# Two layers' gate rows and rotary half-swap moved from constant-matrix products to DMA

## The chip, the cores and the metric

The kernel runs on one NeuronCore of a Trainium2 chip, as one program. The metric is the device time of one execution in microseconds; lower is better. All arithmetic is in 32-bit floats. The engines named here are TensorE (matrix products), VectorE, ScalarE, SyncE (which issues the weight loads) and the DMA engines.

## The reference

The model has a first block (a Hyena mixer and a gated linear scan side by side, then a mixture of 64 experts) and a second block of two hybrid layers on 256 tokens of width 1024. A hybrid layer projects its normalized input to 21 parts, runs five branches of width 512 on them, gates and merges the branches, projects again and adds the result to its input. Two of the branches are touched here.

The mLSTM branch has 4 heads of width 128. Per head and token it has a row of gate values, from a running sum `bcum` of the log of the forget gate and a running maximum:

```
bcum = cumsum(log_sigmoid(f));  m_t = bcum + cummax(i - bcum)       (chunk by chunk in the reference)
log_d[t, s] = bcum[t] - bcum[s] + i[s] - m_t[t]
sc[t, s] = (q[t] . k[s]) * d**-0.5 * exp(log_d[t, s])   for s <= t
h[t] = sum_s sc[t, s] v[s] / max(|sum_s sc[t, s]|, exp(-m_t[t]))
```

The term `bcum[t] - m_t[t]` depends on the query's token alone, and so does `exp(-m_t[t])`. The kernel holds scores with keys on the partitions and queries along the free dimension, so both of these rows have to be present on all 128 partitions.

The retention branch turns its queries and keys by a rotary embedding before it forms scores with a fixed decay:

```
rotary(t):  t1, t2 = t[..., :64], t[..., 64:]
            concat(t1 * cos - t2 * sin,  t1 * sin + t2 * cos)
```

In the kernel the 128 places of a head are the partitions, so the rotation needs each half of the partitions to see the values of the other half.

## The kernel before

Activations lie with the feature on the partitions and the 256 tokens along the free dimension. A projection to 128 columns is a strip: 8 products of 128x128 weights with 128x256 activations into one bank of PSUM (line 518). Values (`ml_v`, `rt_v` and others) are projected with tokens on the partitions instead, 128x512 at a time (line 531). A unit is 4 strips of weights, 2 MB, and SyncE loads it into one of three slots as soon as the unit three places earlier has been used (line 485).

Strips are numbered as jobs. Jobs take PSUM banks 0 and 1 in turn, and a strip starts only when the one two places before it has been taken out of its bank (`evacuated(pe, j - 2)`). For `ml_o`, `rt_q`, `rt_k`, `rt_v` and `gm_u` ScalarE takes it out (function `take`, line 774, and line 878). For `ml_z`, `rt_z` and `gm_z` ScalarE computes an exponential (`exp_neg`, line 780), and VectorE's function `gate` (lines 956 to 962) adds one, takes the reciprocal and multiplies; its last operation frees the bank.

The order of work on each engine is written out by hand in one function for each engine (`layers_pe`, `layers_act`, `layers_dve`), with semaphores between them. Both layers run the same code. Around the change TensorE's order in a layer is:

- `ml_v` 0, the input and forget gates (line 645), `ml_v` 1, the strips `ml_o` 0 to 3, a turn of the gate values into columns (line 651), then the strip `ml_z` 0.
- The front of head 0, then `ml_z` 1, 2 and 3. A front (`ml_front`) is a product of the 4 gate rows with the constant `sel` (4x128, a row of ones for one head), which puts that head's two rows on all partitions of a PSUM bank (line 666), and a pair of causal products of keys and queries into the next bank (lines 563 and 564).
- A loop over the heads: front of the next head, strip `rt_q`, sums over values and over ones (lines 568 and 569), strip `rt_k`.
- `rt_v` 0, the head norm's sums (line 687), `rt_v` 1.
- Four products with the constant `rot`, 128x128, with entries -1 and 1, on two heads of `rt_q` or `rt_k` each (line 699). They give the swapped and signed halves in four PSUM banks.
- The strips `gm_u` 0 and 1, then, when VectorE's rotation has finished, the first retention front (`rt_front`, again lines 563 and 564), `gm_u` 2 and 3, and a loop over the heads like the one above.
- The merge of the five branches: 80 gate and branch products in pairs (lines 731 and 737), and the output projection (line 752).

VectorE computes the gate rows (lines 1096 to 1105) while TensorE is in `ml_v` 1 and `ml_o`. Between the gates of `ml_z` 0 and `ml_z` 1 it forms the weights of head 0 (lines 1116 and 1117 read the broadcast row from PSUM, ScalarE takes the exponential at line 886, line 1119 multiplies by the scores). In the loop it forms the next head's weights and then the current head's quotient (lines 1130 to 1133), where the broadcast `exp` row comes from a copy that ScalarE makes of it (`ml_exm`, line 889). The scaling by the head norm follows (lines 1137, 1138), and then the rotation: four times a product with the sine into a buffer `rt_t`, a product with the cosine in place and a sum (lines 1147 to 1149). The sine and cosine (`rope`) are computed once in the first block, from the positions and the constant `inv_freq`.

All constants of this kind lie in one block `const` of 1121.5 KB, loaded at the start (line 1275), behind the input and ahead of the first weights.

Of the kernel before, what the change touches and what calls it, by code (L numbers as in the profile page):

```python
# [7 lines left out]
F32 = mybir.dt.float32  # L8
I32 = mybir.dt.int32
ALU = mybir.AluOpType  # L10
# [86 lines left out]
def shape_constants():  # L97
# [7 lines left out]
    rot = np.zeros((P, P))  # L105
    rot[np.arange(64) + 64, np.arange(64)] = -1
    rot[np.arange(64), np.arange(64) + 64] = 1
    c.add("rot", rot)
# [7 lines left out]
    c.add("inv_freq", np.concatenate([inv, inv])[:, None])  # L116
    sel = np.zeros((4, 4, P))
    sel[np.arange(4), np.arange(4)] = 1
    c.add("sel", sel.reshape(4, -1))
# [151 lines left out]
def build_program(nc, d, spot):  # L271

    with ExitStack() as ctx:
# [112 lines left out]
        rt_q, rt_k, rt_v = ly.take(4, SEQ), ly.take(4, SEQ), ly.take(2, HALF)  # L386
        ly.at = kept_at + 2 * KD * SEQ
# [44 lines left out]
        ml_w, ml_exm = lw.take(2, 3 * P), lw.take(2, SEQ)  # L432
# [3 lines left out]
        ml_sum = lw.take(2, 4)  # L436
        assert lw.at <= (RING - RING2) * WSLOT
        lw = Layout(spare, r_three)
        rt_t = lw.take(2, 2 * SEQ)
# [57 lines left out]
        def layers_pe(pe):  # L497
            for plan in plans:
# [156 lines left out]
                w("mg_e", 1, 1)  # L655
# [101 lines left out]
        def layers_act(act):  # L757
# [3 lines left out]
            for plan in plans:  # L761
# [117 lines left out]
                w("mg_r", 2, 2)  # L879
# [1389 lines left out]
```

## Time and profile before

| | |
|---|---|
| median of 3 runs | 2385.25 us (2384.37 to 2386.61) |
| profiled execution | 2390.79 us |
| its span, first to last instruction | 2389.0 us |
| TensorE products busy | 2026.9 us, 85% |
| TensorE weight loads busy | 1365.8 us, 57% |
| VectorE busy | 891.4 us, 37% |
| ScalarE busy | 282.4 us, 12% |
| data moved | 592.23 MB, mean 248 GB/s |
| mean granted TensorE clock | 0.935 of full speed |

The span is that of the profiled execution, which is a single one and is 5.5 us above the median of the timed runs. Its time is 1.8 us more than its span. The first block up to the experts takes the first slices, the expert stage lies between some 300 and 1262 us, and the two hybrid layers follow to the end. In the trace a 32-bit product appears as two records, so 8 products of a kind are counted as 16. The records of products overlap by the length of the pipeline; the time that a piece of work takes on TensorE is read from the difference of two start times.

### The profile page before, as it was taken

What the parts mean: (1) busy time and instruction counts of PE and PEld (TensorE: products, weight loads), DVE (VectorE), ACT (ScalarE), POOL (GpSimd) and SP (SyncE); (2) the same over time, 40 slices, a digit from 0 to 9 for tenths busy, and PEclk for the clock granted to TensorE, in tenths of its full rate; (3) what the DMA queues carried; (4) which work ended last, traced back from release to release, by engine and by line L of the source; (5) the groups of instructions that cost most, each with busy time, mean ns of one, the idle gap of its engine ahead of it and who ended that gap; (6) DMA issues with size and microseconds to landing.
All of it is one profiled execution on the core that took longest, in us unless ns stands there. A gap on an engine that the chain in (4) does not pass through costs nothing. (4 is left out here: it accounts for less than half of the span.)

```text
span 2389.0 us, 24442 instructions
## 1 busy us (share of the span) xinstructions
PE 2026.9 (85%) x10208; PEld 1365.8 (57%) x10208; DVE 891.4 (37%) x1479; ACT 282.4 (12%) x632; POOL 0.2 (0%) x4
## 2 busy tenths in 40 slices
PE   7999976767766666666668999999999999999998
PEld 5576752323322222222225877788885877788887
DVE  5446431111111111111113454465543244466553
ACT  1102210000000000000002221110002222111001
POOL 0000000000000000000000000000000000000000
PEclk9999988898988878888888999999999999999999
DMA  6122189999999999999994332334444233234442
GB/s 232 71 92 73 76 357 427 429 427 428 428 427 429 429 426 429 429 428 430 428 429 194 129 119 106 132 133 158 140 178 161 106 141 141 106 115 157 141 151 88
DMA packets 45194, 592.23 MB, mean 248 GB/s; under 512 B 5463, under 2 KB 6904, under 8 KB 7800
## 3 DMA queue, kind: packets, MB, share of 16 engines
q1 hardware_dynamic: 43672, 585.34, 60.9%
q10 hardware_dynamic: 1440, 5.70, 0.7%
q8 instruction: 63, 1.03, 0.2%
q14 instruction: 19, 0.16, 0.0%
HBM read 589.98 MB, written 1.05 MB: 247 GB/s over the span
## 5 line engine op out<-in xcount | busy, mean ns | idle before, releaser
L518 PE MATMUL ps<-arena,ring 128*128 128x256 f32 x1856 | 413.8, 378 | 0.1
L518 PEld LDWEIGHTS ps<-arena,ring 128*128 128x128 f32 x1856 | 345.7, 189 | 50.6 <-issue 2.9
L1591 PE MATMUL ps<-ring,arena 128*32 128x512 f32 x2048 | 250.8, 635 | 91.4 <-DMA ring<-in_w_experts 72.0
L731 PE MATMUL ps<-arena,ring 128*128 128x256 f32 x1280 | 289.2, 378 | 0.0
L1618 PE MATMUL ps<-ring,arena 128*32 128x512 f32 x1024 | 175.2, 818 | 118.1 <-DMA ring<-in_w_experts 113.4
L731 PEld LDWEIGHTS ps<-arena,ring 128*128 128x128 f32 x1280 | 241.5, 189 | 35.6 <-issue 1.0
L1591 PEld LDWEIGHTS ps<-ring,arena 128*32 128x32 f32 x2048 | 63.3, 113 | 260.2 <-issue 140.3
L1618 PEld LDWEIGHTS ps<-ring,arena 128*32 128x32 f32 x1024 | 33.2, 130 | 242.6 <-DMA ring<-in_w_experts 162.8
L737 PE MATMUL ps<-arena,ring 128*128 128x256 f32 x640 | 151.8, 379 | 0.3
L1578 PE MATMUL ps<-arena 128*128 128x128 f32 x512 | 90.6, 359 | 67.2 <-DVE arena L2124 67.2
L1176 DVE RECIPROCAL arena<-arena 128x256 f32<-128x256 f32 x80 | 140.3, 1753 | 2.8
L2139 DVE COPY arena<-ps 128x512 f32<-128x512 f32 x32 | 20.6, 686 | 306.7 <-PE ps L1618 306.7
L1338 PE MATMUL ps<-arena,ring 128*128 128x272 f32 x512 | 126.4, 404 | 6.6 <-DVE arena L1826 4.0
L737 PEld LDWEIGHTS ps<-arena,ring 128*128 128x128 f32 x640 | 121.0, 189 | 18.4 <-issue 1.0
L1578 PEld LDWEIGHTS ps<-arena 128*128 128x128 f32 x512 | 87.6, 271 | 73.4 <-DVE arena L2124 73.4
L1338 PEld LDWEIGHTS ps<-arena,ring 128*128 128x128 f32 x512 | 98.8, 195 | 33.1 <-DVE arena L1826 4.5
L1175 DVE TENSOR_SCALAR arena<-arena 128x256 f32<-128x256 f32 x80 | 23.6, 295 | 176.0 <-ACT arena L929 176.0
L1623 PE MATMUL ps<-arena 128*128 128x256 f32 x256 | 68.4, 426 | 22.5 <-DVE arena L2139 22.5
L1623 PEld LDWEIGHTS ps<-arena 128*128 128x128 f32 x256 | 53.5, 215 | 52.6 <-DVE arena L2139 44.2
L929 ACT ACTIVATE arena<-ps 128x256 f32<-128x256 f32 x80 | 30.8, 385 | 380.1 <-PE ps L731 374.4
L959 DVE RECIPROCAL arena<-arena 128x256 f32<-128x256 f32 x40 | 70.1, 1753 | 1.4
L531 PE MATMUL ps<-ring,arena 128*128 128x512 f32 x160 | 70.3, 593 | 0.0
(385 smaller groups left out, 1739.6 us busy)
## 6 DMA issues: line engine op xcount, KB each, us to landing
ring<-in_w_experts SPq DMA_DIRECT2D x192, 2048.0 KB, 25.5
ring<-in_w_layers SPq DMA_DIRECT2D x42, 2048.0 KB, 7.8
ring<-in_w_layers SPq DMA_DIRECT2D x40, 1536.0 KB, 6.5
ring<-in_w_first SPq DMA_DIRECT2D x10, 2048.0 KB, 8.3
arena<-in_w_mem SPq DMA_DIRECT2D x2, 2048.0 KB, 11.1
arena<-in_mem ACTq DMA_DIRECT2D x2, 1024.0 KB, 6.9
arena<-in_fourier SPq DMA_DIRECT2D x1, 1544.0 KB, 20.8
arena<-in_gm_rows ACTq DMA_DIRECT2D x2, 768.0 KB, 4.6
```

Source lines behind the costliest of these rows:

```text
L518: last = pe.matmul(ps[:, j % 2, 0:SEQ], t[:, s, k, :], lhs[:, k, :], start=(k == 0), stop=(k == KD - 1))
L531: last = pe.matmul(ps[:, bank_of(name, j), :], lhs[:, k, m * P:(m + 1) * P], t[:, :, k, :], start=(k == 0), stop=(k == KD - 1))
L731: last = pe.matmul(ps[:, j % 2, 0:SEQ], t[:, k, :], an[:, k, :], start=(k == 0), stop=(k == KD - 1))
L737: last = pe.matmul(ps[:, (j + 1) % 2, 0:SEQ], t[:, KD + k, :], y_all[:, n, k, :], start=(k == 0), stop=(k == 3))
L929: act.activation(esig[:, p % 2, :], ps[:, j % 2, 0:SEQ], ACT.Exp, scale=-1.0).then_inc(sem(f"job_out{j % 2}"), 1)
L959: link(dve.reciprocal(e, e))
L1176: link(dve.reciprocal(e, e))
L1338: last = pe.matmul(out, w[:, k, :], a[:, k, :], start=(k == 0), stop=(k == KD - 1))
L1578: last = pe.matmul(ps[:, 4 + k // 4, (k % 4) * P:(k % 4 + 1) * P], xn[:, tt, k * P:(k + 1) * P], onehot[:, tt, :], start=(tt == 0), stop=( ...
L1591: last = pe.matmul(ps[CAP * e:CAP * (e + 1), v // 4, :], xg[:, (v % 4) * 2 + k, CAP * e:CAP * (e + 1)], w[:, k, e, :], start=(v % 4 == 0 a ...
L1618: last = pe.matmul(ps[CAP * e:CAP * (e + 1), 2 + half, :], mid_t[:, v - 8, CAP * e:CAP * (e + 1)], w[:, e, half * 512:(half + 1) * 512], s ...
L1623: last = pe.matmul(ps[:, 4 + k // 2, (k % 2) * SEQ:(k % 2 + 1) * SEQ], y_slot[:, k * P:(k + 1) * P], back, start=True, stop=True)
```

## The change

The constants `rot` and `sel` go, with the products that use them (lines 666 and 699) and ScalarE's copy `ml_exm`.

In their place ScalarE sends, behind the evacuation of `ml_o` 0, the 4 x 512 gate rows to a buffer in DRAM, and behind that of `ml_o` 2 it waits for this transfer and issues a second one, which reads the 2048 values back on every one of the 128 partitions (`ml_all`, 1 MB). VectorE reads the rows from `ml_all` for the weights and for the quotient. TensorE's first front moves from ahead of `ml_z` 1 to behind it, and VectorE's and ScalarE's work for head 0 moves by one gate in the same way.

For the rotation ScalarE issues, once the last `rt_k` is out of its bank, two transfers from SBUF to SBUF of 512 KB each: partitions 64 to 127 of `rt_q` and `rt_k` to partitions 0 to 63 of `rt_turned`, and the other way round. VectorE's rotation works on `rt_turned`; the sign is now in `inv_freq`, whose first half is negative. TensorE waits for the rotation one strip later, behind `gm_u` 2. All new transfers are on ScalarE's queue.

```diff
-    c.add("rot", rot)
-    c.add("inv_freq", np.concatenate([inv, inv])[:, None])
-    c.add("sel", sel.reshape(4, -1))
+    c.add("inv_freq", np.concatenate([-inv, inv])[:, None])
...
+        rt_qk = arena[:, kept_at:kept_at + 8 * SEQ]
...
+        ml_all = lw.take(4, 2 * SEQ)
+        rt_turned = lw.take(8, SEQ)
+        ml_rows_out = nc.dram_tensor("ml_rows_out", (LAYERS, 4, 2 * SEQ), F32, kind="Internal").ap()
...
                 def ml_front(hd):
-                    at = 2 + 4 * (hd % 2)
-                    sel = C("sel", 4).rearrange("p (h m) -> p h m", h=4)[:, hd, :]
                     if hd >= 2:
-                        w("ml_dx", 2 * NH, 2 * hd - 2)
-                        w("ml_exm", NH, hd - 1)
                         w("ml_s", NH, hd - 1)
-                    pe.matmul(ps[:, at, :], sel, ml_rows[0:4, :], start=True, stop=True)
-                    causal_pair(ps[:, at + 1, :], lambda kt: ml_k[:, hd, kt * P:(kt + 1) * P], ml_q[:, hd, :]).then_inc(sem("mb_ps"), 1)
+                    causal_pair(ps[:, 3 + 4 * (hd % 2), :], lambda kt: ml_k[:, hd, kt * P:(kt + 1) * P], ml_q[:, hd, :]).then_inc(sem("mb_ps"), 1)
+                strip("ml_z", 1)
                 ml_front(0)
-                strip("ml_z", 1)
                 strip("ml_z", 2)
...
-                unit_evacuated(pe, plan, "rt_q")
-                unit_evacuated(pe, plan, "rt_k")
                 w("ml_h", NH, NH)
-                for i, src in enumerate((rt_q, rt_q, rt_k, rt_k)):
-                    pe.matmul(ps[:, 2 + i, :], C("rot"), xr(src[:, 2 * (i % 2):2 * (i % 2) + 2, :]), start=True, stop=True).then_inc(sem("rr_ps"), 1)
...
                 strip("gm_u", 1)
+                strip("gm_u", 2)
                 w("rt_rot", 4, 4)
                 rt_front(0)
-                strip("gm_u", 2)
...
                     act.activation(ml_o[:, i, :], ps[:, j % 2, 0:SEQ], ACT.Exp, scale=-1.0).then_inc(sem(f"job_out{j % 2}"), 1)
-                w("mg_r", 2, 2)
-                act.activation(ml_rows[0:4, SEQ:2 * SEQ], ml_rows[0:4, SEQ:2 * SEQ], ACT.Exp).then_inc(sem("mg_e"), 1)
+                    if i == 2:
+                        w("ml_rows_out", 16, 16)
+                        act.dma_start(xr(ml_all), ml_rows_out[l].rearrange("a b -> (a b)").partition_broadcast(P)).then_inc(sem("in_ml_all"), 16)
+                    if i == 0:
+                        w("mg_r", 2, 2)
+                        act.activation(ml_rows[0:4, SEQ:2 * SEQ], ml_rows[0:4, SEQ:2 * SEQ], ACT.Exp).then_inc(sem("mg_e"), 1)
+                        w("mg_e", 1, 1)
+                        act.dma_start(ml_rows_out[l], ml_rows[0:4, :]).then_inc(sem("ml_rows_out"), 16)
...
-                    if hd >= 2:
-                        w("ml_h", NH, hd - 1)
-                    act.copy(ml_exm[:, hd % 2, :], ps[:, 2 + 4 * (hd % 2), SEQ:2 * SEQ]).then_inc(sem("ml_exm"), 1)
                 exp_neg("ml_z", 0)
+                exp_neg("ml_z", 1)
                 ml_decays(0)
-                for i in range(1, 4):
+                for i in range(2, 4):
                     exp_neg("ml_z", i)
...
+                unit_evacuated(act, plan, "rt_q")
+                unit_evacuated(act, plan, "rt_k")
+                for half in range(2):
+                    act.dma_start(xr(rt_turned)[64 * half:64 * half + 64, :], rt_qk[64 - 64 * half:128 - 64 * half, :]).then_inc(sem("in_turned"), 16)
                 take("rt_v", 0, rt_v[:, 0, :])
...
-                    dve.scalar_tensor_tensor(x[:, 0:SEQ], ps[:, at, 0:SEQ], ml_col[:, hd:hd + 1], LC("causal_neg"), ALU.add, ALU.add).then_inc(sem("ml_dx"), 1)
+                    dve.scalar_tensor_tensor(x[:, 0:SEQ], ml_all[:, hd, 0:SEQ], ml_col[:, hd:hd + 1], LC("causal_neg"), ALU.add, ALU.add).then_inc(sem("ml_dx"), 1)
...
                 gate("ml_z", 0, y_all[:, 1])
+                gate("ml_z", 1, y_all[:, 1])
+                w("in_ml_all", 16, 16)
                 ml_weights(0)
...
-                    link(dve.scalar_tensor_tensor(r, den, -1.0, ml_exm[:, hd % 2, :], ALU.mult, ALU.max))
+                    link(dve.scalar_tensor_tensor(r, den, -1.0, ml_all[:, hd, SEQ:2 * SEQ], ALU.mult, ALU.max))
...
-                for i, src in enumerate((rt_q, rt_q, rt_k, rt_k)):
-                    s = src[:, 2 * (i % 2):2 * (i % 2) + 2, :]
-                    w("rr_ps", 4, i + 1)
-                    t = rt_t[:, i % 2, :].rearrange("p (h t) -> p h t", h=2)
-                    tick(dve.tensor_tensor(t, ps[:, 2 + i, :].rearrange("p (h t) -> p h t", h=2), rope[:, 0:1, :].to_broadcast([P, 2, SEQ]), ALU.mult))
+                w("in_turned", 32, 32)
+                for i in range(4):
+                    t, qk = (v.rearrange("p (h t) -> p h t", t=SEQ)[:, 2 * i:2 * i + 2, :] for v in (xr(rt_turned), rt_qk))
+                    tick(dve.tensor_tensor(t, t, rope[:, 0:1, :].to_broadcast([P, 2, SEQ]), ALU.mult))
```

## Rows read from the trace of the kernel before

**Rows 1.** The page, part 2: what the DMA engines moved in each fortieth of the span.
```profile
GB/s 232 71 92 73 76 357 427 429 427 428 428 427 429 429 426 429 429 428 430 428 429 194 129 119 106 132 133 158 140 178 161 106 141 141 106 115 157 141 151 88
```

**Rows 2.** Windows: length, busy us (instructions) by engine, TensorE's clock, DMA share, GB/s.
```profile
core 0: us, PE busy (x) PEld busy (x) DVE busy (x) ACT busy (x) POOL busy (x), PEclk, DMA share, GB/s
1450.00:1512.00 62.00, 61.94 (x270) 47.73 (x269) 28.68 (x44) 9.64 (x27) 0.00 (x0) 1.00 0.35 129
1600.00:1800.00 200.00, 200.00 (x928) 174.94 (x927) 101.25 (x140) 16.72 (x45) 0.00 (x0) 1.00 0.46 158
1995.00:2140.00 145.00, 144.94 (x617) 110.84 (x615) 72.27 (x108) 28.91 (x58) 0.00 (x0) 1.00 0.29 105
```

**Rows 3.** Timeline of TensorE, mLSTM part of layer 0: start, us, line, operands, count.
```profile
1450.90 3.72 PE L518 MATMUL ps<-arena,ring 128*128 128x256 f32 x16
...
1456.36 10.85 PE L518 MATMUL ps<-arena,ring 128*128 128x256 f32 x48
1467.14 1.12 PE L666 MATMUL ps<-ring,arena 4*128 4x512 f32 x2
...
1468.95 3.62 PE L518 MATMUL ps<-arena,ring 128*128 128x256 f32 x16
...
1483.83 3.62 PE L518 MATMUL ps<-arena,ring 128*128 128x256 f32 x16
1487.38 1.12 PE L666 MATMUL ps<-ring,arena 4*128 4x512 f32 x2
```

**Rows 4.** Timeline of TensorE, from the last `rt_k` on, layer 0.
```profile
1505.62 7.03 PE L531 MATMUL ps<-ring,arena 128*128 128x512 f32 x16
...
1521.07 3.60 PE L699 MATMUL ps<-arena 128*128 128x512 f32 x8
1524.51 7.07 PE L518 MATMUL ps<-arena,ring 128*128 128x256 f32 x32
1531.42 0.59 PE L563 MATMUL ps<-arena 128*128 128x256 f32 x2
...
1532.07 7.07 PE L518 MATMUL ps<-arena,ring 128*128 128x256 f32 x32
```

**Rows 5.** Timeline of VectorE in the same stretches of layer 0.
```profile
1438.04 0.40 DVE L1105 SCALAR_TENSOR_TENSOR ring<-ring 4x256 f32<-4x256 f32 x1
...
1458.09 0.47 DVE L1116 SCALAR_TENSOR_TENSOR ring<-ps,ring,arena 128x256 f32<-128x256 f32 x1
...
1459.41 0.55 DVE L1119 TENSOR_TENSOR ring<-ring,ps 128x384 f32<-128x384 f32 x1 [0.59 <-ACT ring L886]
1460.43 0.30 DVE L956 TENSOR_SCALAR arena<-arena 128x256 f32<-128x256 f32 x1 [0.47 <-ACT arena L780]
...
1463.01 0.42 DVE L962 TENSOR_TENSOR arena<-ps,arena 128x256 f32<-128x256 f32 x1
...
1517.97 1.23 DVE L1138 TENSOR_TENSOR arena<-arena 128x1024 f32<-128x1024 f32 x1
1522.13 0.69 DVE L1147 TENSOR_TENSOR ring<-ps,arena 128x512 f32<-128x512 f32 x1 [2.93 <-PE ps L699]
...
1529.61 0.69 DVE L1149 TENSOR_TENSOR arena<-arena,ring 128x512 f32<-128x512 f32 x1
```

**Rows 6.** Timeline of ScalarE: evacuations of `ml_o` 0 and of `rt_k` 3.
```profile
1440.11 0.38 ACT L878 ACTIVATE ring<-ps 128x256 f32<-128x256 f32 x1 [2.87 <-PE ps L518]
...
1505.82 0.37 ACT L774 COPY arena<-ps 128x256 f32<-128x256 f32 x1 [4.39 <-PE ps L518]
```

**Rows 7.** DMA issues: queue, count, KB each, median us from issue to landing.
```profile
arena<-in_mem ACTq DMA_DIRECT2D x2, 1024.0 KB, 6.9
...
out<-arena SPq DMA_DIRECT2D x4, 256.0 KB, 2.2
```

**Rows 8.** The start: load of the constants, ScalarE's squares, and TensorE's first wait.
```profile
arena<-in_const SPq DMA_DIRECT2D x1, 1121.5 KB, 8.0
...
5.83 2.02 ACT L256 ACTIVATE arena<-arena 128x2176 f32<-128x2176 f32 x1 [3.81 <-DMA arena<-in_h]
...
PE ps L261 <- DMA arena<-in_const: 9.4, 1, 9.4
```

More of the change, by code:

```diff
@@ L104, in shape_constants @@
     c.add("notbefore", i[:, None] >= i[None, :])
-    rot = np.zeros((P, P))
-    rot[np.arange(64) + 64, np.arange(64)] = -1
-    rot[np.arange(64), np.arange(64) + 64] = 1
-    c.add("rot", rot)
     c.add("keymask", np.concatenate([i[:, None] < np.arange(SEQ)[None, :], i[:, None] < i[None, :]], axis=1))
@@ L115, in shape_constants @@
     inv = (np.float32(10000.0) ** (-(np.arange(half, dtype=np.float32) / np.float32(half)))).astype(np.float32)
-    c.add("inv_freq", np.concatenate([inv, inv])[:, None])
-    sel = np.zeros((4, 4, P))
-    sel[np.arange(4), np.arange(4)] = 1
-    c.add("sel", sel.reshape(4, -1))
+    c.add("inv_freq", np.concatenate([-inv, inv])[:, None])
     c.add("run", np.broadcast_to((np.arange(T) % CHH != 0)[None], (P, T)))
@@ L431, in build_program @@
         ml_rows = lw.take(2 * SEQ)
-        ml_w, ml_exm = lw.take(2, 3 * P), lw.take(2, SEQ)
+        ml_w = lw.take(2, 3 * P)
         ml_den = lw.take(2, SEQ)
@@ L436, in build_program @@
         ml_sum = lw.take(2, 4)
+        ml_all = lw.take(4, 2 * SEQ)
+        rt_turned = lw.take(8, SEQ)
+        ml_rows_out = nc.dram_tensor("ml_rows_out", (LAYERS, 4, 2 * SEQ), F32, kind="Internal").ap()
         assert lw.at <= (RING - RING2) * WSLOT
         lw = Layout(spare, r_three)
-        rt_t = lw.take(2, 2 * SEQ)
         rt_w = lw.take(2, 3 * P)
@@ L1110, in ml_weights @@
                 def ml_weights(hd):
-                    at, x = 2 + 4 * (hd % 2), ml_w[:, hd % 2, :]
-                    w("mb_ps", NH, hd + 1)
+                    at, x = 3 + 4 * (hd % 2), ml_w[:, hd % 2, :]
                     if hd >= 2:
                         w("mo_ps", NH, hd - 1)
-                    dve.scalar_tensor_tensor(x[:, 0:SEQ], ps[:, at, 0:SEQ], ml_col[:, hd:hd + 1], LC("causal_neg"), ALU.add, ALU.add).then_inc(sem("ml_dx"), 1)
-                    dve.scalar_tensor_tensor(x[:, SEQ:3 * P], ps[:, at, P:SEQ], ml_col[:, 4 + hd:5 + hd], LC("causal_neg")[:, 0:P], ALU.add, ALU.add).then_inc(sem("ml_dx"), 1)
+                    dve.scalar_tensor_tensor(x[:, 0:SEQ], ml_all[:, hd, 0:SEQ], ml_col[:, hd:hd + 1], LC("causal_neg"), ALU.add, ALU.add).then_inc(sem("ml_dx"), 1)
+                    dve.scalar_tensor_tensor(x[:, SEQ:3 * P], ml_all[:, hd, P:SEQ], ml_col[:, 4 + hd:5 + hd], LC("causal_neg")[:, 0:P], ALU.add, ALU.add).then_inc(sem("ml_dx"), 1)
                     w("ml_de", NH, hd + 1)
-                    dve.tensor_tensor(x, x, ps[:, at + 1, 0:3 * P], ALU.mult).then_inc(sem("ml_s"), 1)
+                    w("mb_ps", NH, hd + 1)
+                    dve.tensor_tensor(x, x, ps[:, at, 0:3 * P], ALU.mult).then_inc(sem("ml_s"), 1)
                 gate("ml_z", 0, y_all[:, 1])
+                gate("ml_z", 1, y_all[:, 1])
+                w("in_ml_all", 16, 16)
                 ml_weights(0)
-                for i in range(1, 4):
+                for i in range(2, 4):
                     gate("ml_z", i, y_all[:, 1])
@@ L1141, in layers_dve @@
                 head_scale(ml_q, "mlh", y_all[:, 1], "ml_y")
-                for i, src in enumerate((rt_q, rt_q, rt_k, rt_k)):
-                    s = src[:, 2 * (i % 2):2 * (i % 2) + 2, :]
-                    w("rr_ps", 4, i + 1)
-                    t = rt_t[:, i % 2, :].rearrange("p (h t) -> p h t", h=2)
-                    tick(dve.tensor_tensor(t, ps[:, 2 + i, :].rearrange("p (h t) -> p h t", h=2), rope[:, 0:1, :].to_broadcast([P, 2, SEQ]), ALU.mult))
-                    link(dve.tensor_tensor(s, s, rope[:, 1:2, :].to_broadcast([P, 2, SEQ]), ALU.mult))
-                    dve.tensor_tensor(s, s, t, ALU.add).then_inc(sem("rt_rot"), 1)
+                w("in_turned", 32, 32)
+                for i in range(4):
+                    t, qk = (v.rearrange("p (h t) -> p h t", t=SEQ)[:, 2 * i:2 * i + 2, :] for v in (xr(rt_turned), rt_qk))
+                    tick(dve.tensor_tensor(t, t, rope[:, 0:1, :].to_broadcast([P, 2, SEQ]), ALU.mult))
+                    link(dve.tensor_tensor(qk, qk, rope[:, 1:2, :].to_broadcast([P, 2, SEQ]), ALU.mult))
+                    dve.tensor_tensor(qk, qk, t, ALU.add).then_inc(sem("rt_rot"), 1)
                     w("rt_rot", 4, i + 1)
```

2 lines of the change are left out of this document (removed).

## The prediction

> **What bounds the kernel now.** I read the page's slices first: the DMA rate stands at 427 to 430 GB/s from the sixth to the twenty-first slice, the expert stage, and at a third of that and less behind it [rows 1]. So the experts are bound by loads, and what follows is not. Then the windows of the two hybrid layers. The reader is to see there that TensorE is busy 61.94 of 62 us in the stretch with the mLSTM, all of 200 us in the merge that follows, and 144.94 of 145 us in the same stretch of layer 1, always at a granted clock of 1.00 (2.4 GHz), while VectorE, ScalarE and the DMA engines are far from full [rows 2]. So in the layers TensorE alone sets the end, and what it no longer has to do comes off the time, one for one, unless a new wait takes its place. Third, the timeline of TensorE over the instructions that the diff takes out, because there the price of each is a difference of two start times. Last, VectorE and ScalarE beside them, to see how late a transfer may land.
>
> **Units of the sum.** A plain strip is 3.455 us (two of them lie between 1524.51 and 1531.42) [rows 4]. The front of a retention head, a pair of causal products and nothing else, takes 1532.07 - 1531.42 = 0.65 us [rows 4].
>
> **The row broadcast leaves TensorE.** Now a front of an mLSTM head takes 1468.95 - 1467.14 = 1.81 us, the `sel` product with it [rows 3]. Without the product it is a retention front: 0.65 us. The strip ahead of a `sel` product is also longer, 1487.38 - 1483.83 = 3.55 against 3.455, 0.10 us [rows 3]. One `sel` product thus costs 1.26 us, and there are 4 in each layer, 8 in all. For heads 2 and 3, in the middle of the loop, I take all of it: 2.52 us a layer.
> Around heads 0 and 1 the gates of `ml_z` interfere. From the start of `ml_z` 0 to that of `rt_q` 0 it is 1468.95 - 1450.90 = 18.05 us [rows 3]. In it the three strips from 1456.36 to 1467.14 take 10.78 where 3 x 3.455 + 0.10 = 10.47 is due: 0.31 us of waiting. The place is `ml_z` 3, which needs the bank of `ml_z` 1, and that gate ends at 1463.01 + 0.42 = 1463.43 [rows 5]. In the new order: `ml_z` 0 with its present start-up 3.55, `ml_z` 1 3.455, front 0 0.65, strips 2 and 3 6.91, front 1 0.65: 15.2 us, so `rt_q` 0 could start at 1466.1. Its wait is for the gate of `ml_z` 2. Gate 1 now starts behind a strip that ends 1457.9, plus 0.3 and ScalarE's 0.4: 1458.6, and lasts 3.0 (1460.43 to 1463.43): 1461.6. The weights of head 0 are behind it, 1458.09 to about 1459.96, 1.9 us with ScalarE's exponential in their middle [rows 5]: 1463.5. Gate 2 then takes 3.0: 1466.5, and with the handshake `rt_q` 0 starts about 1466.6. That is 0.6 us of waiting in place of 0.31. The stretch falls from 18.05 to 15.8 us: 2.2 us. The unknown here is the order of ScalarE's work: below, no wait (0.6 more a layer); above, the exponential of gate 2 behind that of the weights, another 0.5.
>
> **The rotation leaves TensorE.** The four `rot` products lie from 1521.07 to 1524.51, 3.44 us, back to back [rows 4]. They go whole: TensorE has no wait in front of them.
>
> **Is the broadcast there in time?** ScalarE sends the rows after the evacuation of `ml_o` 0 at 1440.11 + 0.38 [rows 6]; with the exponential (0.4) and the issue (0.5) that is 1441.4. VectorE's part must be ready by then; its last operation on the rows ends at 1438.04 + 0.40 [rows 5], so this wait costs nothing. A store of 256 KB lands 2.2 us after issue [rows 7]; this one has 8 KB and is taken at the same 2.2: 1443.6. ScalarE asks for it two strips after 1440.11, at 1447.4: 3.8 us of room. Behind that wait stand the evacuation of `ml_o` 3 and then `ml_col`; TensorE would feel them only at `ml_z` 1. The broadcast of 1 MB is issued at 1447.4 and read by VectorE at 1461.6: 14.2 us. The same size on the same queue landed in 6.9 us as the median of two [rows 7]; taken: 7. The nearest worse case is that the 2 MB unit issued at 1450.4 goes wholly before it: 2.1 MB at 427 GB/s, 4.9 us [rows 1], so 12 us. Both ends cost nothing. If it did come later, VectorE's queue holds gate 2, for which TensorE already waits, so every microsecond beyond 14.2 is lost at once.
>
> **Are the turned parts there in time?** Let E be the end of `rt_k` 3, now 1505.62 [rows 4]. ScalarE copies it 0.2 us later for 0.37 [rows 6], then issues two transfers of 512 KB: E + 1.5. VectorE is at that time waiting for the norm of the mLSTM; the scaling ends at 1517.97 + 1.23 = 1519.20, E + 13.6 [rows 5]. The rotation takes 1529.61 + 0.69 - 1522.13 = 8.2 us [rows 5], nearly the same with an operand in SBUF (0.68 against 0.69 in the rows). TensorE reaches the first retention front at E + 15.45 (to 1521.07) + 3 strips = E + 25.8. So landing by E + 17.5 costs nothing, 16 us after issue. Expected: the loads for the slots of `rt_q` and `rt_k` are issued at about E - 4.8 and E, 4.2 MB together; at 427 GB/s they and the 1 MB take 12.3 us from about E - 2.8: E + 9.5 at the latest for a fair share, and E + 3.7 + 5 = E + 8.7 if alone. Then the rotation runs from E + 13.6 to E + 21.8, 4 us ahead of TensorE (now 1530.30 against 1531.42: 1.1 us). Bounds of the added wait: 0 at this rate, and no upper end from any row, since no copy from SBUF to SBUF is in the trace; the nearest is the slowest rival below.
> The transfers of rows 7 touch all 128 partitions, and no row shows one between halves. The Trainium skill says in "SBUF — State Buffer", section "Door 1: The DMA port swizzle", that a range of 64 partitions reaches only half the ports, measured there at 196 GB/s, and that two transfers to opposite halves serialize. By that, an estimate: 1.05 MB in 5.4 us instead of 2.5, landing up to 3 us later, about E + 12.5, still before VectorE is free. By the rule the sum is the same; what it takes is a part of the room.
> The weight loads that share with these transfers have a slot free more than ten microseconds before use, so a delay of 2.5 to 5 us does not reach TensorE.
>
> **The smaller constant block.** 128 + 512 columns leave `const`: 320 of 1121.5 KB. TensorE's first product waits for it until 9.4 us [rows 8]. At 427 GB/s that is 0.77 us; the bounds are 0 (if what is queued beside it fills the gap) and 1.5 (ScalarE's squares, ready at 5.83 + 2.02 = 7.85, bound next [rows 8]). Taken: 0.8. Everything behind in the first block hangs on that chain and moves with it.
>
> **Other edits.** ScalarE loses 8 short copies; four DMA issues of 0.5 us fall into gaps of 3 us: nothing. The sign in `inv_freq` is data.
>
> **Sum.** A layer: 2.2 + 2.52 + 3.44 = 8.2 us; two layers 16.4; start 0.8: 17.2 us. The profiled execution took 2390.79 (span 2389.0 and 1.8 around it), so 2373.6 for it. It lies 5.5 above the median of the runs, 2385.25; from that the forecast is 2368.0 us, 0.7% faster.
>
> **Rivals.**
> (1) VectorE's gate chain becomes the bound in the mLSTM part. For it: TensorE already waits 0.31 us there and each gate holds VectorE 3.0 of a strip's 3.455. Then the 4 fronts of each layer turn into waits, and only rotation and start are left, 6.9 + 0.8: 2377.5. Against it: in the loop over heads VectorE has one quotient and one set of weights, about 5 us, in what will be 8.9 us.
> (2) The broadcast is late, 3 us beyond its 14.2 (two trips through DRAM and a unit load beside it): 6 us back, 2374. Against: 1 MB never needed that long in the layers.
> (3) Slower than before: the exchange between halves of SBUF is not spread over the 16 DMA engines. Its price is in the stretch before the first retention front. On one engine, 427/16 = 26.7 GB/s, 1.05 MB takes 39.3 + 2.2 = 41.5 us, 25.3 beyond the 16.2 of room; twice: 50.6 lost, 2418.6. It decides from 24.4 us after issue on, where the 8.2 gained in a layer are gone. For it: no row shows such a copy. Against: rows of 8 KB on 64 partitions look like every other transfer, and all of those share the engines.
> (4) It does not do what it says: the waits take just what the products cost, for instance a landing near 24 us. About 2385. Nothing speaks for this exact size.
>
> **How the numbers follow.** Forecast 0.79, with a range of its own of 2365 to 2371; rival 1 0.07; rival 2 0.06; rival 3 0.04; rival 4 0.04. About 0.2%, 5 us, is what a measurement here can tell from no change. Faster: 0.79 + 0.07 + 0.06 = 0.92, of which I move 0.01 to slower for what isn't listed: 0.91; same 0.04; slower 0.05. The range goes down to 2363.5 (no wait at `rt_q` 0, 1.2; 0.6 more at the start; the rest is the spread of the runs, 2.2) and up to 2377.5, which takes rivals 1 and 2 in.
>
> **What would show it.** In the profile after: no products of 4 x 512 and no rotation products; fronts of 0.65 us; a gap of about 0.6 us ahead of `rt_q` 0; `rt_v` 1 followed at once by `gm_u`; the broadcast landing in 5 to 9 us and the two exchange transfers in 5 to 11; VectorE's rotation beginning right behind the scaling, not behind a DMA; the first product at 8.6 us. Wrong would be TensorE idle ahead of the first retention front, or VectorE's first weights released by a DMA.

## The result, and the profile after

The changed kernel takes 2367.32 us (median of 4 runs, 2366.11 to 2370.99), the kernel before 2385.56 in the same session. The ratio is 0.9925, with a 95% interval from 0.9914 to 0.9937: 18 us, or 0.75%, faster. The forecast was 2368.0, and 17.2 us. Two later sessions gave 2371.08 against 2386.65 (0.9934, 0.9917 to 0.9951) and 2369.59 against 2387.43 (0.9929, 0.9915 to 0.9943), so the gain is 16 to 18 us.

The profiled execution took 2367.8 us, with a span of 2366.0. In its timeline TensorE has lost the products of 4x512 and of the rotation. The mLSTM part of layer 0 answers to [rows 3]:

```profile
1442.62 7.17 PE L514 MATMUL ps<-arena,ring 128*128 128x256 f32 x32
1449.63 0.59 PE L559 MATMUL ps<-arena 128*128 128x256 f32 x2
...
1457.19 0.59 PE L559 MATMUL ps<-arena 128*128 128x256 f32 x2
1457.62 0.38 PE L560 MATMUL ps<-arena 128*128 128x128 f32 x2
1458.11 3.69 PE L514 MATMUL ps<-arena,ring 128*128 128x256 f32 x16
...
1492.36 7.03 PE L527 MATMUL ps<-ring,arena 128*128 128x512 f32 x16
...
1500.94 7.03 PE L527 MATMUL ps<-ring,arena 128*128 128x512 f32 x16
1507.81 10.52 PE L514 MATMUL ps<-arena,ring 128*128 128x256 f32 x48
1518.17 0.59 PE L559 MATMUL ps<-arena 128*128 128x256 f32 x2
1518.82 3.62 PE L514 MATMUL ps<-arena,ring 128*128 128x256 f32 x16
```

From `ml_z` 0 to `rt_q` 0 it is now 1458.11 - 1442.62 = 15.49 us, where it was 18.05. A front of 0.65 from 1457.19 ends at 1457.84, so TensorE waits 0.27 us for the gate of `ml_z` 2. The loop over the heads lasts 1492.36 - 1458.11 = 34.25 us, where it was 36.67 (1505.62 - 1468.95 in [rows 4] and [rows 3]). `gm_u` follows `rt_v` 1 at once. In layer 1 one thing is different: a gap of 1.81 us ahead of the first retention front, in TensorE's timeline:

```profile
2068.18 10.52 PE L514 MATMUL ps<-arena,ring 128*128 128x256 f32 x48
2080.51 0.70 PE L559 MATMUL ps<-arena 128*128 128x256 f32 x2 [1.81 <-DVE arena L1143]
```

VectorE's timeline shows why, layer 0 first and then layer 1. The rotation no longer begins behind the scaling (line 1133) but behind a DMA:

```profile
1504.71 1.23 DVE L1133 TENSOR_TENSOR arena<-arena 128x1024 f32<-128x1024 f32 x1
1509.40 0.69 DVE L1141 TENSOR_TENSOR ring<-ring,arena 128x512 f32<-128x512 f32 x1 [3.47 <-DMA ring<-arena]
...
1516.90 0.69 DVE L1143 TENSOR_TENSOR arena<-arena,ring 128x512 f32<-128x512 f32 x1
...
2065.07 1.23 DVE L1133 TENSOR_TENSOR arena<-arena 128x1024 f32<-128x1024 f32 x1
2072.26 0.69 DVE L1141 TENSOR_TENSOR ring<-ring,arena 128x512 f32<-128x512 f32 x1 [5.96 <-DMA ring<-arena]
```

In layer 0 the rotation ends at 1517.59, 0.6 us ahead of TensorE; in layer 1 it is late. Both rows with DMA in them are what the prediction didn't expect, and TensorE's gap in layer 1 is its own sign of being wrong. The issues and landings of the new transfers (issue row, then its time to landing in layer 0 and in layer 1; then the page's medians for the broadcast and the constants) are:

```profile
L900 ACTq DMA_DIRECT2D ring<-arena x2: 537/574/611, 1493.0 to 1493.6; - x2
DMA to landing us min/median/max: 12.7/14.2/15.8
...
L900 ACTq DMA_DIRECT2D ring<-arena x2: 484/549/614, 2053.4 to 2053.9; - x2
DMA to landing us min/median/max: 12.2/15.3/18.3
...
ring<-ml_rows_out ACTq DMA_DIRECT2D x2, 1024.0 KB, 4.8
...
arena<-in_const SPq DMA_DIRECT2D x1, 801.5 KB, 6.8
```

The broadcast landed 4.8 us after an issue at 1438.7, and VectorE used it at 1453.2. The exchange took 12 to 18 us, and the 2 MB load that SyncE issued 0.5 us ahead of it landed after 16.5 us in layer 0, where the load at the same place took 9.5 before; nothing waited for it. At the start TensorE's first wait ended at 8.12, not 9.37.

### Where the time between the two traces lies

The spans differ by 23.0 us, more than the timed medians, so I set stretches of both side by side. The layers are cut at the first product of the gate projection of each layer, which is the same instruction in every kernel, and at the first product of layer 1.

| stretch, us | before | after | after, 2nd trace | after, 3rd trace |
|---|---|---|---|---|
| start to the gate projection of layer 0 | 1425.91 | 1417.63 | 1422.35 | 1424.81 |
| from there to layer 1 | 387.37 | 378.95 | 378.95 | 378.95 |
| layer 1 to its gate projection | 181.34 | 181.41 | 181.58 | 181.58 |
| from there to the last product | 383.97 | 377.62 | 377.66 | 375.55 |

The two stretches that the change touches are 8.42 and 6.35 us shorter. In the third trace the exchange landed in 15.1 us in both layers, TensorE had no wait in layer 1, and its stretch is 8.42 shorter too. What lies ahead of them spreads by 7 us among executions of one kernel. A part of this is TensorE's granted clock in the first block, in windows of 12 us around the same group of products (columns as in [rows 2]), before, after, and after in its second trace:

```profile
250.00:262.00 12.00, 9.36 (x40) 7.50 (x39) 3.79 (x11) 5.08 (x12) 0.00 (x0) 0.72 0.00 0
```
```profile
246.00:258.00 12.00, 9.36 (x60) 8.07 (x59) 6.51 (x15) 5.87 (x14) 0.00 (x0) 1.00 0.00 1
```
```profile
250.00:262.00 12.00, 9.36 (x42) 7.54 (x41) 3.95 (x11) 4.93 (x12) 0.00 (x0) 0.72 0.00 0
```

The same kernel stands at 1.00 once and at 0.72 once, so the 3 us that this gives are no effect of the change. The place is behind a gap of 2.64 us, which all fourteen traces of this case have: the 16 products behind it take 3.8 us in four of them, 5.2 to 5.5 in three and 6.8 in seven, whatever the kernel.

### The profile page after: what moved, and what is told of

Read it like the earlier page. It is cut to its first block and busy times, and to the rows that moved or that the text cites. A ratio compares the mean times of both kernels' runs of the same rounds, so it can differ in the third digit from the quotient of the medians.

```text
span 2366.0 us, 24364 instructions
## 1 busy us (share of the span) xinstructions
PE 2004.5 (85%) x10176; PEld 1359.0 (57%) x10176; DVE 891.0 (38%) x1479; ACT 279.7 (12%) x624; POOL 0.2 (0%) x4
## 5 line engine op out<-in xcount | busy, mean ns | idle before, releaser
L723 PEld LDWEIGHTS ps<-arena,ring 128*128 128x128 f32 x640 | 121.0, 189 | 18.4 <-issue 1.0
L1617 PE MATMUL ps<-arena 128*128 128x256 f32 x256 | 69.1, 429 | 22.5 <-DVE arena L2133 22.5
L2130 DVE TENSOR_TENSOR arena<-arena,ps 128x512 f32<-128x512 f32 x16 | 11.0, 689 | 159.0 <-PE ps L1585 159.0
## 6 DMA issues: line engine op xcount, KB each, us to landing
arena<-in_w_mem SPq DMA_DIRECT2D x2, 2048.0 KB, 11.2
```

Of the source, the lines that this page charges most:

```text
L723: last = pe.matmul(ps[:, (j + 1) % 2, 0:SEQ], t[:, KD + k, :], y_all[:, n, k, :], start=(k == 0), stop=(k == 3))
L1617: last = pe.matmul(ps[:, 4 + k // 2, (k % 2) * SEQ:(k % 2 + 1) * SEQ], y_slot[:, k * P:(k + 1) * P], back, start=True, stop=True)
```

## The experiments

Theory A was that the gain is what TensorE no longer does, less the idle time that the late exchange gives back. Theory B put a part of it down to the clock ahead of the layers. For the landing of the exchange there were three theories: S, it shares the DMA engines with the unit loads; H, a transfer on 64 partitions is slow by itself; E, it runs on few engines. Where a single execution of a kernel is given, there is no interval.

### The change again, its two parts alone, and the constants

The first is the changed kernel itself.

> The changed kernel as it is, on the chip of the next three. Theory A: the gain is TensorE's products taken off, 8.4 us in each layer by the two traces, less TensorE's idle time ahead of the first retention front (0 in layer 0, 1.9 us in layer 1), plus 1.3 to 2 us at the start; so 18 us below the kernel before, 2367 us, and a trace that shows this idle time in layer 1 again, with the exchange landing 12 to 18 us after issue. Rival B: part of the 18 us is the granted clock in stages that the change does not touch (5 us of the 23 us between the two traces); then this time lies at 2370 to 2372 us, and the idle time may be gone.

Gate rows by DMA alone:

```diff
 # from the changed kernel
...
+    c.add("rot", rot)
-    c.add("inv_freq", np.concatenate([-inv, inv])[:, None])
+    c.add("inv_freq", np.concatenate([inv, inv])[:, None])
...
+                for i, src in enumerate((rt_q, rt_q, rt_k, rt_k)):
+                    pe.matmul(ps[:, 2 + i, :], C("rot"), ...)
...
-                    act.dma_start(xr(rt_turned)[...], rt_qk[...])
...
```

VectorE's rotation reads the products from PSUM again, and TensorE's wait for it stands behind `gm_u` 1 again.

> The gate rows by DMA, the rotation by products as before (its constant and its sign back). Theory A: the stretch from ml_z 0 to rt_q 0 falls from 18.05 to 15.5 us, the loop over the heads from 36.67 to 34.25, both layers: 10.0 us; the constants shrink by 256 KB: 1 us; the time is 11 us below the kernel before, 2374.5 us. Rival B: the wait for the gate of ml_z 2 takes most of it: 8 us or less. With no exchange in flight TensorE has no idle time ahead of the first retention front beyond that of before.

Exchange by DMA alone:

```diff
 # from the kernel before
...
-                    pe.matmul(ps[:, 2 + i, :], C("rot"), ...)
...
+                for half in range(2):
+                    act.dma_start(xr(rt_turned)[...], rt_qk[...])
...
```

The sign in `inv_freq`, VectorE's rotation and the later wait of TensorE go with it; `sel` and its products stay.

> The exchange by DMA, the gate rows by the constant product as before. Theory A: 3.44 us less on TensorE in each layer, less 0 to 1.9 us of idle time where the exchange lands too late, plus 0.2 us for 64 KB of constants: 5 to 7 us below before, 2378.5 to 2380.5 us; with rows_only it adds up to the whole change within 1.5 us. Rival B: the two edits help each other, because the broadcast delays weight loads which then meet the exchange: then the exchange lands clearly sooner here, under 9 us after issue, and no idle time is left.

The constants at their old size:

```diff
+    c.add("unused", np.zeros((P, 5 * P)))
```

> The changed kernel with 640 unused columns in the constant block, so that it has its old 1121.5 KB. Theory A: TensorE's first product waits until 9.3 us instead of 8.1, and all behind it moves: 1.3 us slower than the changed kernel, up to 2 if the clock's rise moves with it. Rival B: the start has no effect that reaches the end, since the expert stage is bound by its loads and the layers wait for it: no difference from the changed kernel. Rival C: what stands in the trace as a shorter stretch at half the clock, late in the first block (4 us earlier between 254 and 260 us), hangs on this block too: then 4 us or more slower.

| | time, us | ratio to before (95%) | layer 0, shorter by | layer 1, shorter by |
|---|---|---|---|---|
| changed kernel | 2371.08 | 0.9934 (0.9917 to 0.9951) | 8.42 | 6.31 |
| rows alone | 2377.34 | 0.9967 (0.9953 to 0.9981) | 4.99 | 4.98 |
| exchange alone | 2380.03 | 0.9972 (0.9961 to 0.9983) | 3.07 | 3.38 |
| constants padded | 2371.20 | 0.9933 (0.9916 to 0.9949) | 8.42 | 8.30 |

Before had 2386.65 here. The changed kernel gave 15.6 us, not the 18 of theory A, and its time lies in rival B's 2370 to 2372; the idle time in layer 1 that theory A named was there. With 17.8 us in the third session, the difference between 16 and 18 is not larger than what sessions differ by.

By the medians the parts give 9.3 and 6.6 us, together 15.9, and the whole gives 15.6. By the ratios, whose intervals reach some 3 us to either side, it is 7.9 and 6.7 against 15.8. They add up as far as the timed runs can tell. In the traces the parts are 10.0 and 6.5 against the 10.0 and 5 to 7 of theory A, and the whole is 14.7, because its exchange was late in layer 1. The time of the rows alone was forecast 11 us below before and was 9.3. The rival of the rows (8 us or less) is refuted by the stretches, not by the timed runs, whose interval reaches from 4.5 to 11.2 us. The rival of the exchange (landing under 9 us without the broadcast) is refuted: it landed after 16.6 and 16.3 us there, and 0.37 and 0.06 us of the 3.44 were missing.

Theory A wanted the padded constants 1.3 us slower. They were not: 2371.20 against 2371.08, as rival B had it. In the trace TensorE's first product waited until 8.83 us, not the 9.3 of theory A, against 8.09 in the changed kernel's trace of the same session, so the block costs 0.7 us there. The exchange of layer 1 landed after 16.4 instead of 18.4 us, which gave back the 2 us of waiting in this one execution; whether the timed runs had the same isn't shown. The reason that rival B gave doesn't hold in the traces: from its first to its last product at line 1591 (line numbers of the kernel before) the expert stage takes 900.7 to 901.8 us in the traces of before, of the changed kernel (three) and of the padded one, so it starts later and ends later by the same. What the start is worth at the end is shown by the first wait alone, and the timed runs don't confirm it. Rival C is refuted: the half-clock stretch is there with and without the padding, and in most traces of the smaller block too.

### Why the exchange lands late

The unit loads held back:

```diff
             for u in range(RING2, len(all_ends)):
                 job_done(sp, all_ends[u - RING2] - 1)
+                for plan in plans:
+                    if u - RING2 in (plan.unit_at["rt_q"], plan.unit_at["rt_k"],):
+                        sp.wait_ge(sem("in_turned"), 32 * (plan.l + 1))
                 layer_unit(sp, u)
```

> The changed kernel, but SyncE issues the two unit loads for the slots of rt_q and rt_k only when the exchange has landed. In the changed kernel the second transfer landed 15.8 us (layer 0) and 18.3 us (layer 1) after its issue, the first 12 to 13. Theory S (sharing: the 16 DMA engines serve the 4.2 MB of weights in turns with it): alone it lands like the broadcast, which took 4.8 us for the same 1 MB: 5 to 6 us after issue, and VectorE's rotation is released by the scaling, not by a DMA. Theory H (halves: a transfer on 64 partitions has half the rate by itself, about 196 GB/s, and the two serialize, as the Trainium skill has it in SBUF — State Buffer, Door 1: The DMA port swizzle): then 7.5 us or more. Theory E (few engines): 14 us or more, as with the loads. The unit loads then land late, so TensorE may wait for one of them at gm_u 0 by up to 2 us a layer.

A copy of full width in place of the exchange:

```diff
-                for half in range(2):
-                    act.dma_start(xr(rt_turned)[64 * half:64 * half + 64, :], rt_qk[64 - 64 * half:128 - 64 * half, :]).then_inc(sem("in_turned"), 16)
+                act.dma_start(xr(rt_turned), rt_qk).then_inc(sem("in_turned"), 16)
...
-                w("in_turned", 32, 32)
+                w("in_turned", 16, 16)
```

This kernel leaves out the change of halves, so its output is wrong; it serves for the time of the transfer alone.

> The changed kernel with the exchange replaced by one copy of the same 1 MB from all 128 partitions to the same 128 partitions, so the halves are not exchanged and the rotation is computed from the wrong half. The unit loads beside it are as in the changed kernel. Theory S (sharing with the loads): lands as late as the exchange, 13 to 17 us after issue, since the bytes and the loads are the same. Theory H (half the partitions, half the rate): lands 3 us or more sooner, 9 to 12 us, and TensorE's 1.8 us ahead of the first retention front of layer 1 are gone.

The exchange twice:

```diff
+                for dst in (ml_all, rt_turned):
                     for half in range(2):
-                        act.dma_start(xr(rt_turned)[...], rt_qk[...])
+                        act.dma_start(xr(dst)[...], rt_qk[...])
...
-                w("in_turned", 32, 32)
+                w("in_turned", 64, 64)
```

> The changed kernel with the exchange made twice, first into the free buffer ml_all, then into rt_turned, 2 MB in four transfers; VectorE waits for all four. From it, what a microsecond of landing costs. Both theories: the room of 16.2 us is used up (0.6 us left in layer 0, nothing in layer 1), so each microsecond later shows as TensorE idle ahead of the first retention front. Theory S: 1 MB more at the full rate, 2.5 us, plus an issue of 1.2: about 3 us idle in layer 0, 5.5 in layer 1. Theory H: 5.4 us more, plus the issue: 6 and 8 us. Theory E (few engines): 10 us and more in each.

The landings in layer 0, and for the full width in both layers, in the order of the texts above:

```profile
L903 ACTq DMA_DIRECT2D ring<-arena x2: 542/576/611, 1498.1 to 1498.7; - x2
DMA to landing us min/median/max: 4.4/5.4/6.3
```
```profile
L899 ACTq DMA_DIRECT2D ring<-arena x1: 532/532/532, 1493.6 to 1493.6; - x1
DMA to landing us min/median/max: 12.2/12.2/12.2
...
DMA to landing us min/median/max: 12.2/12.3/12.3
```
```profile
L901 ACTq DMA_DIRECT2D ring<-arena x4: 542/614/657, 1500.5 to 1502.4; - x4
DMA to landing us min/median/max: 12.9/16.2/22.5
```

With the loads out of the way the last transfer lands after 6.3 us, in layer 1 too, and VectorE's rotation starts right behind the scaling. So most of the 15 to 18 us is the company of the loads (S), and E, which wanted 14 us or more, is refuted. The 6.3 us lie between the bounds of S (5 to 6) and H (7.5 or more). One execution took 2371.53 us. TensorE did not wait for the delayed loads in either layer. The full-width copy in the same company needs 12.3, 3 to 6 less than the exchange, and it leaves no wait in layer 1 (375.54 us for the stretch; one execution took 2366.28 us). That part is H. Both hold: without the loads the last landing comes 9 to 12 us sooner, with full width beside them 3 to 6 us sooner.

The packets of the queue q10, which is ScalarE's, show H by itself. Here are their number, their MB and their share of the 16 DMA engines' time in 24 us of layer 0, for the changed kernel, the one with the loads held and the full-width copy:

```profile
q10 hardware_dynamic: 160, 1.05, 18.4%
```
```profile
q10 hardware_dynamic: 160, 1.05, 19.2%
```
```profile
q10 hardware_dynamic: 144, 1.05, 10.3%
```

The same megabyte holds the engines for 4.4 and 4.6 us in halves, with and without the loads, and for 2.5 us at full width. The rest is S. For 4.3 us after the issue, from 1493.0 to 1497.3, the engines move the loads' packets (queue q1) and none of the exchange's:

```profile
q1 hardware_dynamic: 110, 1.54, 98.2%
```

With the loads held the first packet of the exchange starts 1.2 us after the issue. A full-width copy without the loads was not run.

One execution of the doubled exchange took 2397.49 us, 9.5 above before, whose median is 2387.98 here. The last transfer landed 22.5 us after issue in layer 0 and 26.3 in layer 1, and TensorE waited 7.3 and 11.1 us, above the 6 and 8 of theory H and far above the 3 and 5.5 of S; the 11.1 reach the 10 of theory E, the 7.3 don't. Here is layer 0 by its timeline around the first retention front and its clock in four windows:

```profile
1515.34 10.52 PE L514 MATMUL ps<-arena,ring 128*128 128x256 f32 x48
1533.16 1.22 PE L559 MATMUL ps<-arena 128*128 128x256 f32 x2 [7.30 <-DVE arena L1144]
1534.17 0.63 PE L560 MATMUL ps<-arena 128*128 128x128 f32 x2
1534.60 5.80 PE L514 MATMUL ps<-arena,ring 128*128 128x256 f32 x16
```
```profile
1515.00:1525.00 10.00, 10.00 (x47) 8.57 (x46) 0.08 (x1) 1.33 (x3) 0.00 (x0) 1.00 0.96 292
1525.00:1535.00 10.00, 2.70 (x9) 2.00 (x9) 9.69 (x15) 0.37 (x1) 0.00 (x0) 0.69 0.02 10
1535.00:1545.00 10.00, 10.00 (x41) 8.46 (x40) 1.90 (x5) 4.38 (x5) 0.00 (x0) 0.80 0.37 121
1533.10:1539.00 5.90, 5.84 (x15) 4.76 (x16) 3.14 (x6) 0.00 (x0) 0.00 (x0) 0.50 0.01 1
```

The stretch of layer 0 grew to 389.37, by 10.4 us for a wait of 7.3: behind the wait the products are twice as long (1.22 for 0.59), the granted clock is 0.50, its lower level of 1.2 GHz, from 1533.1 to 1539, and a strip takes 5.6 us for 3.46. Layer 1 grew to 389.12, by 13.6 against 375.54, for a wait of 11.1. So the room of 16 us is real, and a microsecond beyond it costs more than one. It is the place that the prediction's rival 3 named, with another cause and a higher price for each microsecond.

### The exchange in two parts, and the place of the front

```diff
                     take("rt_k", hd, rt_k[:, hd, :])
+                    if hd % 2:
+                        evacuated(act, job("rt_q", hd))
+                        evacuated(act, job("rt_k", hd))
+                        turned, qk = (v.rearrange("p (s h t) -> p s h t", s=2, h=4)[:, :, hd - 1:hd + 1, :] for v in (xr(rt_turned), rt_qk))
+                        for half in range(2):
+                            act.dma_start(turned[64 * half:64 * half + 64], qk[64 - 64 * half:128 - 64 * half]).then_inc(sem(f"in_turned{hd // 2}"), 16)
...
-                w("in_turned", 32, 32)
-                for i in range(4):
+                for n, i in enumerate((0, 2, 1, 3)):
+                    if n % 2 == 0:
+                        w(f"in_turned{n // 2}", 32, 32)
```

> The changed kernel with the exchange in two parts: heads 0 and 1 of rt_q and rt_k when rt_k 1 is out of its bank, heads 2 and 3 where all of it is now; VectorE rotates the first part first. Four transfers of 256 KB a layer. Theory S: the first part lands within 6 us, 17 us before its use; the second has half the bytes in the same company of loads and lands 2 to 4 us sooner, 12 to 14 us after issue, and VectorE needs it only 4 us after the first. VectorE's rotation begins right behind the scaling, TensorE has no idle time there in either layer: 1.8 us below the changed kernel, the layers' two stretches 8.4 us shorter than before both. Rival: the first transfers, now 4 KB long in place of 8, and 13 us earlier, meet other unit loads and delay them, or the issues hold up ScalarE in the loop over the heads: no gain or 1 to 2 us slower.

It took 2370.52 us in its first session (ratio to before 0.9928, 0.9912 to 0.9945); the changed kernel was not timed beside it there. The first part landed in 3.8 us and the second in 11 to 12, where 12 to 14 was expected. In layer 1 VectorE's rotation begins behind the scaling with no gap:

```profile
2066.88 1.23 DVE L1135 TENSOR_TENSOR arena<-arena 128x1024 f32<-128x1024 f32 x1
2068.03 0.69 DVE L1144 TENSOR_TENSOR ring<-ring,arena 128x512 f32<-128x512 f32 x1
```

This row is of its second trace; both have stretches of 378.9 and 375.5 us. The comparison was then repeated with the changed kernel in the same session, together with the front in its old place:

```diff
+                ml_front(0)
                 strip("ml_z", 1)
-                ml_front(0)
 ... and in the same way ml_decays(0) and ml_weights(0), with its wait for the broadcast, ahead of ml_z 1
```

> The changed kernel again, as the measure for the next two on the same chip. In both of its traces so far TensorE waited 1.8 us ahead of the first retention front of layer 1, and the second transfer of the exchange landed 18.3 to 18.4 us after issue there. Expected: the same a third time, and 2369 to 2371 us.

> The exchange in two parts, as before. In its trace the stretch of layer 1 from the gate projection to the end was 375.53 us, against 377.62 and 377.66 in the changed kernel, and that of layer 0 the same 378.94. Theory A (this is the whole difference): 2.1 us below after_third. Rival (the time goes elsewhere, the parts of the program before the layers spread by 5 us from one execution to the next, so that the medians don't show it): between 1 us slower and 1 us faster.

> The exchange in two parts, and the first mLSTM front, VectorE's weights and ScalarE's exponential of head 0 back ahead of ml_z 1, as in the kernel before, while the rows still come by DMA. In the changed kernel the broadcast landed at 1443.5 us, and VectorE used it at 1453.2; in the old place it would be used at 1449.9, still 6 us after landing. Theory A (the later place buys nothing, because the broadcast is early enough for the old one, but costs a longer wait ahead of rt_q 0): the wait moves from rt_q 0 to ml_z 3 and stays 0.2 to 0.5 us; within 0.5 us of swap_early_again. Rival: the weights of head 0 between gates 0 and 1 hold gate 1 up and TensorE at ml_z 3, as they did in the kernel before, by 0.5 us more a layer: 1 us slower. Counter-rival: VectorE's first weights are then released by a DMA and TensorE stands still for more than 1 us in the mLSTM part.

> The changed kernel with the first mLSTM front and its work on VectorE and ScalarE ahead of ml_z 1, as before the change; the exchange stays whole and late. Separates the order of the front from that of the exchange. Theory A: the stretch from ml_z 0 to rt_q 0 is 15.5 us, within 0.3 of the changed kernel, with no DMA in VectorE's waits there, and layer 1 keeps its wait ahead of the retention front of 1.8 us. Rival: 16 us or more, the gates late.

| | time, us | ratio to before (95%) | layer 0 stretch | layer 1 stretch |
|---|---|---|---|---|
| changed kernel | 2369.59 | 0.9929 (0.9915 to 0.9943) | 378.95 | 375.55 |
| exchange in two parts | 2367.56 | 0.9923 (0.9909 to 0.9936) | 378.96 | 375.55 |
| and the front in place | 2369.38 | 0.9931 (0.9917 to 0.9944) | 379.65 | 376.24 |
| front in place alone, one execution | 2377.42 | | 379.65 | 378.41 |

Before had 2387.43 here. The expectation of a wait in the changed kernel a third time was wrong: the last transfer landed after 15.1 us and nothing waited. So the wait comes in some executions, in two of three traces of this kernel and in that of the front in place. The exchange in two parts was the fastest, by 2.0 us, as theory A had it, but the intervals overlap, the runs do too (2366.51 to 2373.12 and 2365.83 to 2369.52), and this trace of the changed kernel has no wait to remove: the stretches of the two are equal. What is shown is that its two traces have no such wait in any layer, and why; that the 2 us in the median come from it is not shown. The 8 us by which the single execution of the front in place lies above the changed kernel's median are not the front's: the profiled execution of the changed kernel took 2373.12 us itself, and of the 4.3 us from there 2.9 lie in layer 1, where the exchange was late.

The front in its old place costs 0.70 us in each layer, TensorE waiting for gate 1 at `ml_z` 3 (the row is of the kernel with both edits, layer 0):

```profile
1455.55 3.72 PE L514 MATMUL ps<-arena,ring 128*128 128x256 f32 x16 [0.76 <-DVE arena L957]
```

No DMA is in VectorE's waits there. So the later place is worth 0.7 us a layer, for the order of the gates, and the broadcast did not need it. The expected difference of 0.5 us at most, and that of 0.3 for the front alone, were too low; the rival of 1 us for both layers was nearer to the 1.4, and for the front alone the rival held (16.3 us from `ml_z` 0 to `rt_q` 0, where it said 16 or more). In the medians it is 1.8 us, with intervals that overlap. Layer 1 of the front in place kept its wait ahead of the retention front, 1.9 us, as expected.

## Why the prediction was right, step by step

- **The bound.** Right: TensorE set the end, and both layers became shorter by the products removed, save for the late exchange in layer 1. It agreed to 0.1 us in the loop (2.52 forecast, 2.42 measured), and the rotation gave its 3.44 in layer 0.
- **The gates around heads 0 and 1.** 2.2 forecast, 2.56 measured. The wait at `rt_q` 0 is 0.27 us and not 0.6. The chain of start times had slack in it: VectorE starts gate 2 at 1454.96, while the weights of head 0 are still ending (1454.49 + 0.56), so that hand-over costs nothing.
- **The broadcast.** Right: issued two strips after the rows, room of 14 us, landed in 4.8 (forecast 7).
- **The exchange's landing.** This step was wrong. The prediction said "E + 9.5 at the latest for a fair share", where E is the end of `rt_k` 3, and that the rotation would start behind the scaling, 4 us ahead of TensorE. Measured in layer 0: E = 1492.36, last landing 1509.4, E + 17.0, against a limit of E + 17.5; in layer 1 E + 19.5, 2 us too late. The sum of bytes at 427 GB/s failed twice: in halves the megabyte holds the 16 engines for 4.4 us instead of 2.5, and beside the loads it does not begin to move for 4.3 us. Even at full width it landed 12.3 us after issue, where the fair share came to about 8. The Trainium skill says in "SBUF — State Buffer", "Door 1: The DMA port swizzle", that 64 partitions reach half the ports, and the trace agrees with it: 4.4 to 4.6 us of the engines' time in halves, 2.5 at full width. The 3 us that the prediction added for it are near what the full-width copy shows (3 to 6), but the landing that they were added to was itself 3 to 4 us too early.
- **The limit.** Right: 16.2 us from the issue to where TensorE begins to wait. Landings of 15.1 and 15.8 cost nothing, 16.4 cost 0.1 us (the padded kernel's layer 1), 18.3 made a wait of 1.8.
- **The loads beside it.** A delay of 2.5 to 5 us was forecast, without a wait. It was 7 us (16.5 for 9.5 in layer 0), and there was no wait.
- **The constants.** 0.8 forecast, with bounds of 0 and 1.5; the first wait fell by 1.25 us between the traces, and by 0.7 with all else equal. In the timed runs the padded block made no difference, so this term is not confirmed in the time.
- **The sum.** 8.2 a layer forecast; 8.42 and 6.3 to 8.4 measured, 14.8 to 16.8 in all. Two errors of opposite sign, 0.3 us of gates and up to 2.1 of exchange, hardly moved it. The products' prices were right for good reasons. That the exchange cost nothing in layer 0 was in part luck: it came 7.5 us after the forecast's E + 9.5, with 0.6 us of room left. Where the wait occurs, the forecast is 2 us too high in layer 1.
- **The rivals.** Rival 1 did not hold, since VectorE kept up with 0.27 us of waiting. Rival 2 failed at a landing of 4.8. Rival 3's place was right and its cause was not; the doubled exchange shows the slower side of it. Rival 4 did not hold either: the one wait that came took 2 us, not 8.

## What to carry to other kernels

Price work that leaves the bounding engine by differences of start times, and add them only after walking through the chain beside it. For a transfer that takes the place of a product, give the room from issue to use first, then the landing in the company that it will really have: here 4.8 us for a megabyte in a quiet stretch, 12 beside the unit loads, 15 to 18 in halves beside them. If the landing comes within a few microseconds of the room, send the part that is ready first ahead: here it costs two more issues a layer, and neither of its traces has the wait. A total that agrees with the forecast doesn't show that its terms do; look for each sign that was named beforehand.

## What the runs showed of the hardware

- Two half-width transfers of 512 KB within SBUF land 4.4 and 6.3 us after issue when alone; beside the unit loads the second lands after 15.1 to 18.4 us. They hold the 16 DMA engines for 4.4 to 4.6 us, a full-width copy of the same megabyte for 2.5.
- The landing varies between executions of one kernel at the same place (layer 1), 15.1 to 18.4 us, and with it a wait of 0 or 1.8 us.
- A wait of TensorE of 7.3 us was followed by products at 1.2 GHz (granted clock 0.50) and cost 3.1 us more than itself; one of 1.8 us left the clock at 1.00 and cost 2.1.
- The stretch ahead of the layers varies by 7 us between executions, in part by half-clock pieces (3.8 or 6.8 us for the same 16 products) in work that no edit touched, so single traces of two kernels can differ by 5 us more than their medians do.
